# Taking the attention output product inside attention, and mixing from loaded products with double-buffered rows

## What is computed

```python
u, q, k, v, qi, ki, wi, g_conv, g_attn = project_inputs(x, w_in, b_in)
y_conv = conv_branch(u_hist, conv_w, conv_b, conv_ln_g, conv_ln_b, w_conv_out)   # ... @ w_conv_out (512 x 1024)
y_attn = jnp.einsum('bsa,ad->bsd', attend(q, k, v, qi, ki, wi), w_attn_out)      # 512 x 1024
mix = jnp.einsum('bsd,de->bse', g_conv * y_conv + g_attn * y_attn, w_out)        # 1024 x 1024
x = layer_norm(DN_ALPHA * x + mix, ln1_g, ln1_b)
ffn = hier_moe(x, router_group_w, router_group_b, router_expert_w, router_expert_b, w_gate, w_up, w_down)
x = layer_norm(DN_ALPHA * x + ffn, ln2_g, ln2_b)
```

## Time and profile before

| | |
|---|---|
| median of 3 runs | 3370.77 us (3362.61 to 3380.25) |
| profiled execution | 3378.07 us, of which the profiled span is 3376.3 us |
| TensorE busy | 2907.7 us, 86% of the span |
| VectorE busy | 1990.7 us, 59% |
| ScalarE busy | 1076.4 us, 32% |
| POOL busy | 850.2 us, 25% |
| stages in that execution | attention to 1940.9 us, mixing from 2090.9 to about 2589.8 us |

### The profile page before, as it was taken

The page is one execution under the profiler, slowest core; times in us unless marked ns, Lnnn a source line. Parts: engine busy times, 40 slices in busy tenths (PEclk is TensorE's granted clock), DMA queues, the critical chain, the costliest instruction groups (busy, mean ns, idle before and its releaser), DMA issues. The chain is left out here.

```text
span 3376.3 us, 45765 instructions
## 1 busy us (share of the span) xinstructions
PE 2907.7 (86%) x15142; PEld 1803.2 (53%) x15143; DVE 1990.7 (59%) x2882; ACT 1076.4 (32%) x1829; POOL 850.2 (25%) x1263
## 2 busy tenths in 40 slices
PE   8999999999856778788877775899996799999988
PEld 6877799999723344445555542344443433333333
DVE  1699223996267878888877537764434434343437
ACT  2111221111366667586866621000000111111112
POOL 3344333233243323131323240013120000000013
PEclk9999999999967888999988987999997799999989
DMA  3323232344300111111100073444341678768437
GB/s 126 102 91 97 88 105 75 109 142 129 106 13 26 35 47 32 38 35 48 45 23 11 23 266 138 170 150 165 124 139 66 229 275 293 264 256 310 157 139 241
DMA packets 238326, 415.48 MB, mean 123 GB/s; under 512 B 29572, under 2 KB 156804, under 8 KB 225354
## 3 DMA queue, kind: packets, MB, share of 16 engines
q1 hardware_dynamic: 180978, 272.79, 23.8%
q0 software_dynamic: 25216, 89.03, 7.9%
q10 hardware_dynamic: 31968, 51.49, 4.2%
HBM read 518.08 MB, written 96.91 MB: 182 GB/s over the span
## 5 line engine op out<-in xcount | busy, mean ns | idle before, releaser
L387 PE MATMUL p_ps_acc<-p_x_hi,p_w_hi 128*128 128x352 f32 (+2 forms) x1480 | 525.5, 355 | 7.2 <-POOL p_w_lo L319 5.2
L387 PE MATMUL p_ps_acc<-p_x_lo,p_w_hi 128*128 128x352 f32 (+2 forms) x1480 | 523.2, 354 | 0.0
L387 PE MATMUL p_ps_acc<-p_x_hi,p_w_lo 128*128 128x352 f32 (+2 forms) x1480 | 523.0, 353 | 0.0
L633 DVE SCALAR_TENSOR_TENSOR p_conv<-p_uh,p_taps,p_conv 128x1024 f32<-128x1024 f32 x240 | 387.0, 1612 | 8.5
L2620 PE MATMUL e_ps_G<-l_wgu,e_xT 128*64 x768 | 340.9, 597 | 23.3 <-issue 11.8
L2622 PE MATMUL e_ps_G<-e_gu_b,e_xT 128*64 128x512 f32 x768 | 341.0, 597 | 0.0
L1022 PE MATMUL q_ps_s<-a_keys,q_q_st 64*128 64x512 f32 (+3 forms) x640 | 175.2, 664 | 174.6 <-DVE q_top L1293 85.5
L387 PEld LDWEIGHTS p_ps_acc<-p_x_hi,p_w_hi 128*128 128x128 f32 (+1 forms) x1480 | 276.9, 187 | 37.4 <-POOL p_w_lo L319 5.9
L387 PEld LDWEIGHTS p_ps_acc<-p_x_lo,p_w_hi 128*128 128x128 f32 (+1 forms) x1480 | 278.4, 188 | 29.0 <-issue 0.5
L1243 DVE TENSOR_SCALAR_CACHE_REDUCE q_junk_dve<-q_sc,q_mid 128x640 bf16<-128x640 f32 (+6 forms) x175 | 247.0, 1411 | 77.6 <-POOL q_mid L1360 75.7
L387 PEld LDWEIGHTS p_ps_acc<-p_x_hi,p_w_lo 128*128 128x128 f32 (+1 forms) x1480 | 277.0, 187 | 27.3
(11 more groups left out here) (426 smaller groups left out, 5007.8 us busy)
## 6 DMA issues: line engine op xcount, KB each, us to landing
l_wgu<-in_w_gate_dram SPq DMA_DIRECT2D x96, 1024.0 KB
l_wgu<-in_w_up_dram SPq DMA_DIRECT2D x96, 1024.0 KB
l_wd<-in_w_down_dram SPq DMA_DIRECT2D x96, 1024.0 KB
p_w<-in_w_in_dram SPq DMA_DIRECT2D x72, 512.0 KB, 3.9
yb<-e_y SPq DMA_DIRECT2D x48, 512.0 KB
x_gates<-featT SPq DMA_DIRECT2D x64, 256.0 KB, 6.9
featT<-p_stage ACTq DMA_DIRECT2D x28, 528.0 KB
featT<-p_stage ACTq DMA_DIRECT2D x28, 512.0 KB
```

What stands on the lines that cost most here:

```text
L387: m = nc.tensor.matmul(acc[slot][tb][0:rows, 0:width], wp[:, slot, k, 0:rows], xp[:, k, at], start=(k == 0 and i == 0), stop=(k == KD - 1 ...
L633: ch.mark(nc.vector.scalar_tensor_tensor(dst, src, wt, dst, ALU.mult, ALU.add))
```

## The change

1. Attention takes the output product itself. The turned outputs stay on chip (`oT_st`, now three tiles), laid out by head so that they serve as the operand of a product. For each pair of tiles p (256 tokens) there are 8 products, one for each 128 features f: `outputs_in(g)` puts one into each of the slots 10 to 61 and two into slots 62 and 63, ahead of `turn(g, 1)` and of the second part of the next scores; the last pair's 8 (`LAST_PAIR`) come after the last slot. ScalarE copies each product, loads weights ahead (two buffers of 128 x 512; six once the conv products are done), and stores results to `bT` in HBM. SP's stores of `oT` go.
2. `o_raw` and `o_sb` lose their second buffer.
3. Mixing loads `aT` and `bT` in `prods` and needs no branch product: `mixed(b, f)` on VectorE multiplies both with their gates. `mT` has two buffers, and block b + 1's rows are formed during block b's items, two ahead of each item's places 0 and 1. The 8 places behind the branch products are gone; an item has four instead of two (`places(b, m)`): in front of `out(n, 0)`, in front of `out(n, 1)`, behind it, and behind `turn(n - 1, ...)`.
4. SP loads `xt` of item 0 and the gate rows 4 to 7 of block 0 ahead of the router's weights; the second mask always goes to a bank of its own.

```diff
+def outputs_in(g):
+
+    p, f = divmod(g - 10, 8)
+    if g >= 62:
+        return [(6, 2 * (g - 60)), (6, 2 * (g - 60) + 1)]
+    return [(p, f)] if p >= 0 else []
...
+def weights_in(i):
+
+    return i % 2 if i <= LAST_CONV else (i - LAST_CONV - 1) % 6
...
-        o_raw = ph.sb("o_raw", [P, 2, 4, P])
-        o_sb = ph.sb("o_sb", [P, 2, 4, P])
-        oT_st = ph.sb("oT_st", [P, 2, 4, P])
+        o_raw = ph.sb("o_raw", [P, 4, P])
+        o_sb = ph.sb("o_sb", [P, 4, P])
+        oT_st = ph.sb("oT_st", [P, 3, 4, P])
...
+                def product(key):
+                    n, i = at.turns[key], NUMBER[key]
+                    kind, p, f = key
                     bank_free(n)
...
+                    pe.wait_ge(w_loaded[weights_in(i)], 16 * (turn_of(i) + 1))
...
+                        pe.wait_ge(t_kept, at.kept[at.turns["o", 2 * p + 1]])
+                        for x in range(2):
+                            for k in range(CB):
+                                m = nc.tensor.matmul(ps_t[n % 3][:, x * P:(x + 1) * P], w_blk[weights_in(i)][:, k, :], oT_st[:, (2 * p + x) % 3, k, :],
+                                                     start=(k == 0), stop=(k == CB - 1))
...
                     turn(g, 0)
+                    for pf in outputs_in(g):
+                        product(("a",) + pf)
                     if g + 1 < NSLOT and length(nxt) > 1024:
                         scores(g + 1, 1)
                     turn(g, 1)
...
                 turn_raw(NT - 1)
                 turn_out(NT - 1)
+                for pf in LAST_PAIR:
+                    product(("a",) + pf)
...
+                def keep_product(key):
+                    n, i = at.turns[key], NUMBER[key]
+                    width = 512 if key[0] == "c" else 2 * P
+                    for q, stores in staged_before(i):
+                        act.wait_ge(prod_stored[q], 16 * stores)
                     act.wait_ge(t_full, n + 1)
...
+                    for j in next_in(i):
+                        load_product(j)
+                    store_product(i - 1)
...
                     keep_turned(g, 0)
                     count_y(g, 0)
+                    for pf in outputs_in(g):
+                        keep_product(("a",) + pf)
                     keep_turned(g, 1)
...
+        def places(b, m):
+
+            if m == 4:
+                return [None] * 4
+            return [16 * b + 4 * m + i if (b, m) != (LAST_BLOCK, 3) or i < 2 else None for i in range(4)]
...
                     for m, t in enumerate(items[b]):
                         r = rows_of(t)
-                        sample(place_of(b, m, 0))
+                        for pos in places(b, m)[0:3]:
+                            sample(pos)
                         pool.wait_ge(var_ready, n + 1)
                         nc.gpsimd.tensor_tensor(mv[0:r, 1:2], mv[0:r, 1:2], eps[0:r], ALU.pow).then_inc(rstd_ready, 1)
-                        sample(place_of(b, m, 1))
+                        sample(places(b, m)[3])
...
+                    pe.wait_ge(m_done, 8 * b + 8)
+                    for m, t in enumerate(items[b]):
+                        at = places(b, m)
+                        sample(at[0])
+                        if t == NT:
+                            sample(at[1])
+                        out(n, 0)
+                        if n >= 2:
                             route(n - 2)
...
+                        if t != NT:
+                            sample(at[1])
                         out(n, 1)
-                        if m:
+                        sample(at[2])
+                        if n:
                             turn(n - 1, 0)
                             turn(n - 1, 1)
-                        sample(place_of(b, m, 1))
+                        sample(at[3])
...
+                def mixed(b, f):
+                    if b == NB:
+                        return
+                    i = 8 * b + f
+                    row = mT[:, b % 2, f, :]
+                    if b >= 2:
+                        dve.wait_ge(c_full, 4 * (b - 1))
+                    dve.wait_ge(g_loaded[i % GS], 48 * (i // GS + 1))
+                    ch.mark(nc.vector.tensor_tensor(t1[:], prods[:, i % GS, 0], gates[:, i % GS, 0, :], ALU.mult))
+                    ch.link(nc.vector.tensor_tensor(row, prods[:, i % GS, 1], gates[:, i % GS, 1, :], ALU.mult))
+                    nc.vector.tensor_tensor(row, t1[:], row, ALU.add).then_inc(m_done, 1)
+                    dve.wait_ge(m_done, i + 1)
+
                 n = 0
+                for f in range(KD):
+                    mixed(0, f)
...
+                        if m < 4:
+                            mixed(b + 1, 2 * m)
+                        sample(at[0])
+                        if m < 4:
+                            mixed(b + 1, 2 * m + 1)
+                        sample(at[1])
+                        if n >= 2:
                             logit(n - 2)
-                        sample(place_of(b, m, 0))
+                        sample(at[2])
                         dve.wait_ge(c_full, n + 1)
```

305 lines of the change are left out of this document (134 added, 171 removed).

## The result

The changed kernel takes 3409.99 us (median of six runs, 3400.91 to 3417.28), the kernel before 3370.6 in the same series: the ratio is 1.0107 (95% interval 1.0093 to 1.0121). It is slower by 1.1%, 39 us, where no change (3369, within 3353 to 3387) had been forecast. The profiled execution took 3400.91 us, the least of the six, and that of before 3378.07, 7 us over its median; so the two traces differ by only 22.9 us of span, and some 16 us of the difference of the medians cannot be placed in them. What follows splits the 22.9.

What follows compares the result with a forecast made beforehand. Attention was taken as a ring of engines waiting for each other, late mixing as bound by TensorE. Attention +45.5 and mixing -47.6 sum to -2.1 us: 3369 us on the runs' scale, range 3353 to 3387.

Steps and rivals of the forecast that it cites:

- A product's size: Attention: one output product of 16 TensorE instructions takes 1.75 us with loads and matmuls overlapped, 3.7 us as upper bound.
- rival 3: Attention: weight loads are not hidden behind 128-column matmuls, 1.9 us more for each of 64 products, about 3450 us; chance 0.04.
- Slots 15 to 46: Attention, 32 slots waiting ahead of the second scores: +14 for products outlasting shorter waits, -10 for a warmer clock.
- what sticks out of them sums to 15.9 us: Attention: 16 of 32 waits are shorter than a 1.75 us product; the excess is 15.9 us, taken as +14.
- that gives back 8 x 1.25: -10: Attention: products fill eight waits of 3.2 to 4.3 us, so the scores behind run at a faster clock, -10 us.
- The wait for q_top: Attention: TensorE's wait for VectorE's q_top ahead of the second scores was to fall from 81 to near 40 us.
- Mixing up to the mask: Mixing until the sample's mask is ready: VectorE decides, its search rounds standing four to an item; +8 us.
- Mixing behind the mask: Mixing after the sample's mask: TensorE decides; -93.6 us for work and waits that go, +38 for new waits.
- Slow clock after the three long waits: +4: Mixing behind the mask: TensorE's clock is slow after three long waits for gathered rows, +4 us, part of the +38.
- term (a): Mixing behind the mask: waits for v gathers with two buffers, three times 6.5 us and twice 0.8, given as +22.
- Rival 1: Attention: each product goes straight into TensorE's chain, slots before 54 lengthening over 0.7 us each; 3403 to 3418 us; chance 0.23.
- rival 4: Mixing gives little, -25 us, as gathers land late and block 1's rows come later than 2137; 3392 us; chance 0.10.

## Why the prediction was wrong

The forecast was "no change" by a sum of -2.1 us; in the trace's own terms the sum came out as 62.2 - 30.1 = +32.1. The mechanisms it named are nearly all there, and most terms hold:

- **A product's size**, 1.75 us: measured 1.79 from slot 54 on and 1.8 to 2.0 in most slots before, but 3.2 to 3.7 in slots 35, 36 and 41 to 45, at a granted clock of 0.50 to 0.59. The estimate of 4.6 us by the Trainium skill ("TensorE: Matmul & The Clock Gate", "Back-to-back issue gap") and rival 3 are out: each of the sixteen instructions with 128 columns and its own weights takes 3.74/32 = 0.117 us.
- **The end of attention.** Slots 54 and 55 cost 3.0 us (3.5 forecast), slots 56 to 63 22.8 (21), the tail 13.1 (12.5). Slots 10 to 14 and 47 to 53 cost 0.2 (4.5).
- **Slots 15 to 46, where the prediction fell**: 14 - 10 = +4 forecast, +23.1 measured. By stretches that is +2.3 for the products of slots 16 to 23, +12.1 for 24 to 39, +9.6 for 40 to 45 and -0.9 for 46. Two steps failed.

  First, "what sticks out of them sums to 15.9 us", which held a product of 1.75 us to be hidden wherever the wait ahead of the second scores is longer. It failed in slots 41 to 45 (9.0 of the 9.6 us, nothing forecast): the product needs a bank first, and the wait for ScalarE's copy used up the slack ahead of it. I had read who ended the wait, but not what the new instruction itself would wait for. The sixteen slots with a shorter wait, too, cost 22.5 us and not 14; nothing here absorbed what stuck out.

  Second, "that gives back 8 x 1.25: -10". The eight waits of 3.2 to 4.3 us are those of slots 20, 24, 30, 41 to 43, 45 and 46, and the slots changed by -3.0, 0.0, -2.8, +0.8, +2.6, +2.3, +2.5 and -0.9 us: +1.5 in sum. Where the product could start in the wait the mechanism worked: in slot 20 the wait fell from 3.25 to 1.97 us and the scores behind it from 2.08 to 1.13, and the slot's granted clock rose from 0.76 to 0.93, in slot 30 from 0.86 to 1.00.

```profile
1310.70 1.13 PE L1076 MATMUL q_ps_s<-a_keys,q_q_st 64*128 64x512 f32 x4 [1.97 <-DVE q_top L1374]
```

Slot 24 had the full clock before, in spite of its wait of 3.27 us. In slots 41, 42, 43 and 45 the wait for the bank took the old wait's place and the product got the slow clock. These four are 8.2 us longer where 5 us had been counted back; the other four gave 6.8. So the overlooked bank accounts for this term's miss too: slots 41 to 45 are 14 of the 19.1 us by which the stretch passed its forecast. From slot 15 to 24 as a whole the granted clock went from 0.89 to 0.90 only, since what slots 20 and 23 won was partly lost in 18 and 21 (0.92 to 0.86 each). It rose in slots 47 to 53, where nothing had been counted on; windows of before and of after:

```profile
1205.00:1416.00 211.00, 161.69 (x966) 90.77 (x966) 177.88 (x206) 144.31 (x194) 54.24 (x126) 0.89 0.13 41
...
1820.00:1888.00 68.00, 51.22 (x409) 35.99 (x408) 42.92 (x102) 51.34 (x113) 35.24 (x107) 0.87 0.04 9
```

```profile
1204.00:1417.00 213.00, 177.52 (x1105) 107.61 (x1106) 177.77 (x206) 146.94 (x203) 51.00 (x126) 0.90 0.18 54
...
1842.00:1910.00 68.00, 56.38 (x526) 43.55 (x528) 44.27 (x107) 54.45 (x122) 36.21 (x111) 1.00 0.16 47
```

There seven products went by in the same 68 us, and the clock was full.
- **The wait for q_top** ahead of the second scores in slots 15 to 46 fell from 81.1 to 28.6 us, not to 40; but 20.6 us of it only moved in front of the product. The groups of TensorE from 1188 to 1860 us show it in the last columns:

```profile
L1076 PE MATMUL q_ps_s<-a_keys,q_q_st 64*128 64x512 f32 (+3 forms) x456 | 121.8, 651 | 59.8 <-DVE q_top L1374 28.6 <-ACT q_relu L1182 28.4 <-issue 2.7
...
L1139 PE MATMUL q_ps_t<-q_oT_st,q_w_blk 128*128 128x128 f32 x448 | 61.1, 293 | 4.2 <-ACT q_pT L1191 3.9
L1139 PE MATMUL q_ps_t<-q_oT_st,q_y_blk 128*128 128x128 f32 x80 | 17.1, 400 | 16.4 <-ACT q_pT L1191 16.4
```

- **Mixing up to the mask**, +8 forecast, +13.9 measured. The first rows came as forecast (43.8 us against 42 to the first out product); those of block 1 arrived 50.5 us after the start instead of 46.6, which is 3.9 of the 5.9 us.
- **Mixing behind the mask**, -55.6 forecast, -44.0 measured. The gathers' waits were 20.0 us in five (22 forecast), the other new waits 9.3 (12). What was mis-sized is "Slow clock after the three long waits: +4". TensorE's busy time in this part was to be 331.9 - 71.8 - 14 + 1.8 = 247.9 us by the other terms and is 267.9: 20 us, 16 over the forecast, less 4.7 that the waits were under theirs, is the 11.6 missing. The out products of before and after in the TensorE-bound part:

```profile
L2077 PE MATMUL x_ps_AB<-x_wo,x_mT 128*128 128x512 f32 x224 | 99.3, 596 | 1.4 <-DVE x_mT L2264 1.4
```

```profile
L2138 PE MATMUL x_ps_AB<-x_wo,x_mT 128*128 128x512 f32 x192 | 93.0, 641 | 0.0
L2138 PE MATMUL x_ps_C<-x_wo,x_mT 128*128 128x512 f32 x160 | 76.7, 636 | 0.0
```

From 99.3/224 = 0.443 us each to 169.7/352 = 0.482: 14 us over the 352. Not only the out products behind the three long waits (4.0 to 5.9 us) are slow: behind waits of 2.6, 2.7 and 2.9 us they take 8.83, 8.73 and 9.94 instead of 7.1.

Put together: attention came out 16.7 us over its sum, 11.5 by the eight waits whose clock was to be given back, 8.5 by the sixteen short ones, less some 3 elsewhere; mixing gave 17.5 less, 11.6 behind the mask, most of it TensorE's slow clock, and 5.9 up to it, 3.9 of them the late rows. The term (a) of the prediction adds up to 21.1 and not 22, which changes nothing. The Trainium skill's rule (same page, "HAM oscillation") that gaps bring back half clock holds in mixing and in slots 41 to 45; not every gap did so, as slot 24 shows. Rival 1 (3403 to 3418) had the right time by half of its mechanism, which is luck: its threshold of 0.7 us a slot wasn't reached (0.6), and the rest was mixing's shortfall, the mechanism of rival 4.

Open remains why the granted clock falls in slots 18 and 21 while it rises in 20 and 23; and which stages the 16 us between the medians' difference and the traces' lie in, for which the profiled executions give no row.

## What to carry to other kernels

An instruction put into another's wait is free only if it can start when the wait starts: list what the new one waits for itself (here a bank of a ring that another engine empties), not only how long the old wait was. Where a step must be moved, look for the place whose wait ends with something that is far away from it: the loads at the start of a stage hid sixteen products in full. Ahead of the values the six products of slots 41 to 46 cost nothing, but those from slot 56 on 1.35 us each, where the kernel before had waits of only 0.2 to 0.8 us a slot; between the second scores and the second turn each of slots 10 to 53 cost 1.59 of its 1.79 us. And when work between small dependent steps is taken out, the steps move together and their latencies show; spreading them over what is left gave 31 us.
